# A two-layer diffusion backbone on one core: where layer 1's last two modulation chunks are loaded and multiplied

## The reference, cut to what matters

```
mod = (jax.nn.silu(c) @ w_ada[l] + b_ada[l])[:, None, :]
sh1, sc1, gt1, sh2, sc2, gt2 = jnp.split(mod, 6, axis=-1)
h = modulate(rms_norm(x, g_mix[l]), sh1, sc1)
...
x = x + gt1 * merge_branches((o_a, o_b, o_c), (ga, gb, gc), w_branch[l], w_out[l])
x = x + gt2 * expert_choice_ffn(modulate(rms_norm(x, g_ffn[l]), sh2, sc2),
                                w_router[l], w_exp_gate[l], w_exp_up[l], w_exp_down[l])
```

## Time and profile before

| | |
|---|---|
| median of 3 runs | 1928.11 us (1925.49 to 1931.93) |
| the profiled execution's own time | 1932.02 us |
| its span, first to last instruction | 1929.9 us |
| TensorE busy | 1706.7 us, 88% |
| VectorE / ScalarE / GpSimd busy | 802.2 / 497.9 / 110.4 us |
| HBM read | 539.13 MB, mean 281 GB/s over the span |

### The profile page before, as it was taken

One profiled execution on the slowest core, in us unless ns is written; L12 is line 12 of the kernel. 1 busy time (PEld: TensorE's weight loads), 2 busy tenths in 40 slices (PEclk: granted clock), 3 DMA queues, 4 the chain that ended last, 5 costly groups with the idle time before them and its releaser, 6 DMA issues.

```text
span 1929.9 us, 26420 instructions
## 1 busy us (share of the span) xinstructions
PE 1706.7 (88%) x10750; PEld 996.1 (52%) x10750; DVE 802.2 (42%) x1791; ACT 497.9 (26%) x1087; POOL 110.4 (6%) x149
## 2 busy tenths in 40 slices
PE   5999999988998999999998799988798997777865
PEld 2887777766675333333332498867594332222222
DVE  3356666664434233333222656766563221111112
ACT  3225555452123000000000535554342000000001
POOL 1001210000001000000000101300000000000000
PEclk8999999999998999999999899989899999999988
DMA  9332322124687899999999763345478999999996
GB/s 349 125 98 67 104 66 77 34 77 161 231 322 310 342 428 427 428 427 428 428 428 428 245 189 112 98 142 191 163 291 362 427 426 425 426 426 427 426 427 282
DMA packets 149875, 543.82 MB, mean 282 GB/s; under 512 B 9786, under 2 KB 92032, under 8 KB 124156
## 3 DMA queue, kind: packets, MB, share of 16 engines
q1 hardware_dynamic: 147356, 535.98, 70.6%
q0 software_dynamic: 2400, 6.16, 1.1%
HBM read 539.13 MB, written 2.98 MB: 281 GB/s over the span
## 4 chain that ended last, share of the span: by engine, by line
PE 51%; DMA 25%; DVE 13%; ACT 6%; issue 4%; SPq 0%; POOL 0%; DVEq 0%; ACTq 0%
PE bank L1957 19%; PE bank L1821 7%; PE bank L1823 7%; PE bank L1822 7%; DMA ring<-in_w_exp_down 7%; DMA ring<-in_w_exp_up 4%; DMA ring<-in_w_exp_gate 4%; DVE WL L1409 3%; DMA split_slot<-in_w_exp_up 2%; PE bank L1736 2%; DMA split_slot<-in_w_exp_down 2%; DMA split_slot<-in_w_exp_gate 2%; PE bank L1931 2%; DMA ring<-in_w_in 2%; ACT WH L1181 2%
## 5 line engine op out<-in xcount | busy, mean ns | idle before, releaser
L1957 PE MATMUL bank<-ring,XEP 128*32 128x256 f32 (+1 forms) x2576 | 409.1, 620 | 32.6 <-DMA ring<-in_w_exp_up 19.3
L1821 PE MATMUL bank<-HH,WH 128*128 128x512 f32 (+1 forms) x864 | 309.1, 358 | 10.5 <-DVE WL L1409 8.0
L1822 PE MATMUL bank<-HL,WH 128*128 128x512 f32 (+1 forms) x864 | 303.4, 351 | 0.0
L1823 PE MATMUL bank<-HH,WL 128*128 128x512 f32 (+1 forms) x864 | 303.0, 351 | 0.0
L1957 PEld LDWEIGHTS bank<-ring,XEP 128*32 128x32 f32 (+1 forms) x2576 | 120.7, 129 | 290.3 <-issue 238.7
L1409 DVE TENSOR_TENSOR WL<-ring,WH 128x1024 fp32r<-128x1024 f32 (+1 forms) x172 | 185.4, 1079 | 181.7 <-ACT WH L1181 180.9
L1668 DVE TENSOR_TENSOR X<-X,bank 128x512 f32<-128x512 f32 x192 | 119.0, 683 | 192.6 <-PE bank L1976 101.0
L1957 PE MATMUL bank<-ring,HIDT 128*32 128x256 f32 (+1 forms) x1264 | 158.5, 491 | 45.2 <-DMA ring<-in_w_exp_down 45.2
L1181 ACT CAST WH<-ring 128x1024 fp32r<-128x1024 f32 (+1 forms) x172 | 158.1, 925 | 125.0 <-PE bank L1823 57.0
L1821 PEld LDWEIGHTS bank<-HH,WH 128*128 128x128 f32 x864 | 166.6, 193 | 44.2 <-issue 21.0
L1823 PEld LDWEIGHTS bank<-HH,WL 128*128 128x128 f32 x864 | 166.4, 193 | 21.6
(11 more groups left out here) (223 smaller groups left out, 2008.8 us busy)
## 6 DMA issues: line engine op xcount, KB each, us to landing
ring<-in_w_exp_gate SPq DMA_DIRECT2D x57, 2048.0 KB, 30.7
ring<-in_w_exp_up SPq DMA_DIRECT2D x53, 2048.0 KB, 32.3
ring<-in_w_exp_down SPq DMA_DIRECT2D x51, 2048.0 KB, 38.1
ring<-in_w_ada SPq DMA_DIRECT2D x48, 1024.0 KB, 7.6
ring<-in_w_in SPq DMA_DIRECT2D x40, 1024.0 KB, 5.6
split_slot<-in_w_exp_up SPq DMA_DIRECT2D x8, 2048.0 KB, 29.1
split_slot<-in_w_exp_down SPq DMA_DIRECT2D x8, 2048.0 KB, 31.6
ring<-in_w_in SPq DMA_DIRECT2D x28, 512.0 KB, 5.2
```

Of the source, the lines that this page charges most:

```text
L1821: mm(t, wh, hi[:, k, 0:b.n], start=k == 0, stop=False)
L1822: mm(t, wh, lo[:, k, 0:b.n], start=False, stop=False)
L1823: last = mm(t, wl, hi[:, k, 0:b.n], start=False, stop=k == b.kk - 1)
L1957: last = mm(out_bank[tw * g:tw * g + tw, 0:nw], stationary(k), w[:, g::G] if spread else w[:, nw * g:nw * g + nw], start=k == 0, stop=k == ...
```

## The change

In layer 1, `ada(1, 10)` and `ada(1, 11)` go into stage C, behind the `dpair` of `d2` = 1 and of `d2` = 2. The two `window_load` calls behind c4 are gone, and the router step of layer 1 has no late chunks (`s.early` is empty). The layout of `GT2` in layer 1 (four groups of 32 rows, 256 columns) stays, so `ada2` gets a case for it with two adds a chunk, the other half of `SELB`, and a wait for all six `b_ada` rows. Layer 0 is unchanged.

```
-        extra = [] if last else [ada(l, c) for c in (4, 5, 6, 7, 8, 9, 10, 11)]
+        extra = [ada(l, c) for c in ((10, 11) if last else (4, 5, 6, 7, 8, 9, 10, 11))]
         for d2 in range(4):
             atoms = dpair(2, d2)
             mid = len(atoms) // 2
             run(atoms[:mid])
-            if extra:
+            if extra and not last:
                 extra.pop(0)()
             run(atoms[mid:])
             if d2 == 0:
                 P.add("gt2_bias", l=l, sets=P.sets)
                 if last:
                     expert_load(Step(o_ready=("pv_ready", P.sets)))
-            if extra:
+            if extra and (d2 or not last):
                 extra.pop(0)()
...
             for _ in range(3):
                 expert_load(dense_done)
-            late = [window_load(l, c) for c in (10, 11)]
...
-                        late_bank(0)
+                        if s.early:
+                            late_bank(0)
...
-                            dve.wait_ge(gt2_in, 32)
+                            dve.wait_ge(gt2_in, 32 + 64 * l)
                             dve.wait_ge(blk_ready, s.out[0].ready)
+                            if l:
+                                for c in range(2):
+                                    rows = slice(64 * s.half + 32 * c, 64 * s.half + 32 * c + 32)
+                                    last = nc.vector.tensor_tensor(GT2[rows, 0:256], BLK[s.out[0].bank][rows, 256 * c:256 * c + 256], GT2[rows, 0:256], ALU.add)
+                                last.then_inc(dve_evicted, 1)
+                                continue
...
-                            if a.v == GT2V:
-                                if i == 0:
-                                    dve.wait_ge(gt2_in, 32 + 64)
-                                for c in range(2):
-                                    rows = slice(64 * a.half + 32 * c, 64 * a.half + 32 * c + 32)
-                                    nc.vector.tensor_tensor(GT2[rows, 0:256], LATE[i][rows, 256 * c:256 * c + 256], GT2[rows, 0:256], ALU.add)
...
-                            mm(t[:], SELB[:, 1, :], MB[:], start=True, stop=True).then_inc(blk_ready, 1)
+                            mm(t[:], SELB[:, 1 - l, :], MB[:], start=True, stop=True).then_inc(blk_ready, 1)
...
-                            if a.v == GT2V:
-                                last = mm(LATE[i][:], SELB[:, 0, :], MBW[i % 2][:], start=True, stop=True)
...
-                        modulation(s.early[0], (0,))
+                        if s.early:
+                            modulation(s.early[0], (0,))
...
-                        modulation(s.early[0], (1,))
-                        for i in range(1, len(s.early)):
-                            modulation(s.early[i])
-                            turn_late(i - 1)
-                        turn_late(len(s.early) - 1)
+                        if s.early:
+                            modulation(s.early[0], (1,))
+                            for i in range(1, len(s.early)):
+                                modulation(s.early[i])
+                                turn_late(i - 1)
+                            turn_late(len(s.early) - 1)
```

More of the change, by code:

```diff
@@ L1626, in _ @@
                             dve.wait_ge(late_turned, a.turned)
-                            if a.v == GT2V:
-                                if i == 0:
-                                    dve.wait_ge(gt2_in, 32 + 64)
-                                for c in range(2):
-                                    rows = slice(64 * a.half + 32 * c, 64 * a.half + 32 * c + 32)
-                                    nc.vector.tensor_tensor(GT2[rows, 0:256], LATE[i][rows, 256 * c:256 * c + 256], GT2[rows, 0:256], ALU.add)
-                            else:
-                                finish_modulation(a, by_column(LATE[i]), LRED[i], link)
+                            finish_modulation(a, by_column(LATE[i]), LRED[i], link)
                     elif kind == "moe":
@@ L1879, in turn_late @@
                             pe.wait_ge(act_evicted, a.tile.act)
-                            if a.v == GT2V:
-                                last = mm(LATE[i][:], SELB[:, 0, :], MBW[i % 2][:], start=True, stop=True)
-                            else:
-                                for k in range(4):
-                                    last = nc.tensor.transpose(LATE[i][:, 128 * k:128 * k + 128], MBW[i % 2][:, 128 * k:128 * k + 128], IDENT)
+                            for k in range(4):
+                                last = nc.tensor.transpose(LATE[i][:, 128 * k:128 * k + 128], MBW[i % 2][:, 128 * k:128 * k + 128], IDENT)
                             last.then_inc(late_turned, 1)
```

## The result

| | before | changed |
|---|---|---|
| median of 13 runs | 1928.11 us (1924.85 to 1932.85) | 1932.34 us (1928.26 to 1937.71) |
| ratio, 95% interval | | 1.0021 (1.0012 to 1.0030) |
| span of the profiled execution | 1929.9 us | 1930.5 us |

A forecast was written before the change was run, and what follows sets the result against it. The end was taken to follow TensorE's finish of the output stage, which starts the expert stream. Removals, loads and VectorE's work at 0 plus 5.4 us of TensorE products turned 1928.1 into 1933.5 us, range 1929.0 to 1941.0.

The forecast's parts named there:

- What bounds the kernel: Layer 1's end is set by when TensorE's output stage lets the expert stream start, its bytes, and a 20 us tail.
- (a): Four 1 MB loads removed between c4 and c5: c5 waits for line 1832 anyway, so worth 0.
- (b): Router matmuls, bank copies and adds removed: VectorE's top-k is the chain there, so worth 0.
- cold router: Rival: TensorE's clock falls in the emptied router, gather 0.9 us longer plus a few tenths, total 1934.6 us; chance 0.06.
- 2 us to spare: At c10's issue, the expert stream still has some 2 us of earlier bytes to land, so router time gains nothing.
- The added products, 5.4 us: Stage C, TensorE: two chunks at 1.85 us of products plus 0.86 us of selecting product, 5.4 us, all on the path.
- The added work of VectorE and the loads, at 0: Stage C: VectorE's 1.54 us a chunk and the 4.19 MB of loads fit into spare time, priced at 0.
- The slack for the second gate chunk: Stage C: gate weights of d2 = 2 ready at 1409.0 us, needed at 1410.9, slack about 1.9 us.
- The stream that starts earlier: Rival: c5 to c9 follow c4 with 4.19 MB less ahead, 5.4 - 9.9 = -4.5 us, 1923.6 us; chance 0.09.
- Late weights: Rival: in stage C weights come late behind the added loads, 2 to 5 us on top of 5.4; chance 0.16.
- Hidden: Rival: some wait in the output stage takes up the 5.4 us, within 1 us of before; chance 0.07.

The follow-up runs named there:

- e1: Changed kernel without modulation chunks 10 and 11 in layer 1: no loads, products or adds; ratio 1.0005 to the kernel before.
- e4: Changed kernel with the products of chunks 10 and 11 and their selecting products made twice; ratio 1.0054 to the kernel before.
- e5: Kernel before with the b_ada loads and c1 moved behind the weights of d2 = 1 in the DMA queue; ratio 0.9955 to the kernel before.
- e7: Changed kernel with idle products, whose result nobody reads, in the router in place of the late modulation; ratio 1.0030 to the kernel before.
- e8: Changed kernel with six idle 128x512 products ahead of the first gather of layer 1; ratio 1.0056 to the kernel before.
- e2: Changed kernel with the four loads but 4 of 16 product instructions a chunk, no selecting product and no add; ratio 1.0021 to the kernel before.
- e3: Changed kernel with all products of chunks 10 and 11 but without their four loads, reading a constant tile; ratio 1.0038 to the kernel before.
- e6: Changed kernel with the b_ada loads and c1 moved behind the weights of d2 = 1 in the DMA queue; ratio 1.0001 to the kernel before.
- e9: Changed kernel as it is, measured once more; ratio 1.0037 to the kernel before.
- e10: Changed kernel with idle products in the router, measured once more on the same chip as e9; ratio 1.0022 to the kernel before.

## Why the prediction was right

**What bounds the kernel.** The end is set by TensorE's way to line 1832 and the stream behind it. Shown by e1 and e4, which take work out of stage C and put it in: c6 moves by what TensorE gets, and the time follows.

**(a) The removed loads are worth 0.** Shown by e1 and by the 31.2 us wait.

**(b) The removed router work is worth 0.** This held only in part. The chain of the router still waits for VectorE's top-k, but the clock is lower. I had this as the rival of the cold router with 0.06, priced at 0.9 us plus a few tenths for c10, and took it to be covered by 2 us to spare. The price was right: c10 1.43 us later relative to c6, 0.88 in the gather and 0.54 ahead of it. Its cause was right only in part, since the clock falls at the router's start in kernels that keep their products as well (e5, e7) and depends there on more than the change. The room at c10 was right too, 1.9 us by e8. What I overlooked is that the room shrinks behind c10. c12 and what follows wait for products that come after a second gather, and there the kernels whose router has nothing between its own products (changed, e1, e2, e3, e6, e9) move 387 to 403 GB/s, those with products there (before, e5, e7, e10) 424 to 431. That is 0.8 to 1.4 us of the stream. The six and the four lie apart in their traces (e4, whose router is as empty, lies between them at 419, and e8 had its gap earlier); in the medians the loss isn't resolved. That c12's later issue makes the dip is read from the order of events; no run moves it alone. The Trainium skill, TensorE: Matmul & The Clock Gate, What's actually happening, has the throttled clock as the default that activity lifts; the trace agrees, 0.55 on average in the changed router against 0.84.

**The added products, 5.4 us.** Right in kind, 0.4 us too small: 5.76 us measured, 5.80 by the rows. The term took the time from the group's first instruction to the next matmul, 1.85 us, and left out the way in (0.09 us) and the longer first step behind it (0.10 us). The selecting product is 0.86 us, as in layer 0.

**The added work of VectorE and the loads, at 0.** For the loads shown by e3 against the changed kernel, 82.82 and 82.85 us. No run takes VectorE's work out alone; for it stand the unchanged list of waits and the 5.76 us, which TensorE's own rows fill. The slack for the second gate chunk, forecast at 1.9 us, was there; e6 shows what it rested on.

**The total.** The forecast was 5.4 us, 1933.5. The terms that the traces show are 5.8 us and, for the dip in the stream (427 against 403 GB/s over 15 us), 0.9 us, 6.7 in all; but the second isn't seen at the end, where the first profile of the changed kernel takes 0.8 us less from c6 to the output than the kernel before, and e9 1.8 us more. The medians show 4.1 us (2.3 to 5.8) in one comparison and 7.1 us (4.4 to 9.8) in the other, both of the same kernel. They agree with each other and with the forecast; 6.7 us lies above the first interval and within the second. Whether a part of it is given back later in the stream is not settled. The time from c6 to the output varies by 3.5 us among the profiles without e8, and by 2.5 us between the two of the changed kernel, so more profiles would be needed. What was right is the mechanism and the size of the main term; that the total, with 0.4 us missing in that term and the router at 0, falls so close to the medians is in part luck.

**The rivals.** The stream that starts earlier is out (e1). Late weights are out for this kernel, and true for e6. Hidden is out: c6 moves by the whole amount. The cold router is there in the trace, and what it costs the end against the kernel before is smaller than the scatter.

## What to carry to other kernels

A load that is taken out ahead of an idle gap buys nothing: look at what the next request in the queue waited for before counting its bytes. Work that fills an engine's waiting time in one stage is free there, and moved into a stage in which that engine never waits it costs its whole length; here it was VectorE's top-k chain that had made 5.8 us of TensorE's time free. When you price a group of small products, take the distance between its neighbours in the trace and not the group's own duration, and don't divide the duration by the count where they overlap. And read a queue for waits that stand ahead of loads which don't need them: one such line was worth more than the whole change, 8.7 us.

## What the runs showed of the hardware that I had not expected

Sixteen short products over four column groups take 1.92 us, four over two groups 1.05 us. Products on a constant tile in the router, whose result nobody reads, brought the gather from 3.68 us to 1.94 us: the granted clock was at its lower level, 1.2 GHz, at the router's start in both kernels; without them it was so in the gather too, and with them it was at 2.4 GHz there. Two kernels can lie 5.8 us apart in one stage and 0.6 us in the span of their profiles, since the point at which attention ends moves by up to 7.7 us between executions (1376.07 us in e7, 1383.79 in e6) without any change ahead of it.
